# Output projection moved into the layers' stage, its gate's sums formed in the mixing stage, and four tiles leading each layer in units of four row blocks of two tiles

## What is computed

```python
# end of the first block
y = concatenate([ssd_out_norm(...), gdn_out_norm(...)])
h_lat = h_lat + gate_l * rms_norm(y @ w_out, post_w)     # gate_l: the last third of silu(c) @ w_ada + b_ada
# second block, two layers
for l in range(2):
    h = rmsnorm(x, norm_g[l])
    proj = h @ w_in[l]                                   # 7168 columns: v, q, k, g, mq, mg, c, x, s, b tiles
    ...
    x = x + concatenate([y_a, y_d, y_m]) @ w_out[l]
```

## Time and profile before

| what | value |
|---|---|
| median of three runs | 3634.65 us (3633.68 to 3636.38) |
| the profiled execution | 3634.55 us, its span 3632.8 us |
| TensorE busy | 3439.6 us, 95% |
| VectorE / ScalarE / GpSimd busy | 47% / 41% / 9% |
| mean granted TensorE clock | 0.972 |
| recurrent stage's last TensorE work ends | 1530.3 us |
| output projection's products | 1551.0 to 1740.0 us |
| first product of layer 1 / of layer 2 | 1797.1 / 2715.9 us |

### The profile page before, as it was taken

One profiled execution on the slowest core, in us unless ns is written; L12 is line 12 of the kernel. 1 busy time (PEld: TensorE's weight loads), 2 busy tenths in 40 slices (PEclk: granted clock), 3 DMA queues, 4 the chain that ended last, 5 costly groups with the idle time before them and its releaser, 6 DMA issues.

```text
span 3632.8 us, 53291 instructions
## 1 busy us (share of the span) xinstructions
PE 3439.6 (95%) x21996; PEld 2811.6 (77%) x21996; DVE 1712.8 (47%) x2813; ACT 1480.5 (41%) x2296; POOL 318.0 (9%) x334
## 2 busy tenths in 40 slices
PE   7999999999978989799699999999999999999998
PEld 5888888888857878678377777887777777788787
DVE  7665564565525656544744444333234444443422
ACT  6564443344325353232365555222225555632211
POOL 0000230130003323100200000000100000000000
PEclk9999999999989999899799999999999999999999
DMA  9642332333440010165322222333432222233342
GB/s 375 209 143 61 91 101 71 86 105 102 126 163 25 15 49 26 46 212 203 136 87 75 81 83 85 103 99 99 145 104 81 81 81 81 76 104 96 96 139 81
DMA packets 150081, 383.39 MB, mean 106 GB/s; under 512 B 14257, under 2 KB 39089, under 8 KB 149841
## 3 DMA queue, kind: packets, MB, share of 16 engines
q1 hardware_dynamic: 138384, 338.44, 29.5%
q0 software_dynamic: 11456, 41.56, 3.3%
HBM read 350.38 MB, written 29.56 MB: 105 GB/s over the span
## 4 chain that ended last, share of the span: by engine, by line
PE 49%; DVE 1%; ACT 0%; issue 0%; DVEq 0%; POOL 0%; ACTq 0%
PE lay_acc L2478 42%; PE lay_nb L2494 1%; PE lay_sA L2533 1%; PE lay_ob L2551 1%; PE lay_om L2478 1%; PE lay_tb L2512 1%; DVE lay_four L2895 1%; DVE lay_u_lo L2899 0%; PE lay_om L2561 0%; DVE lay_wlo L2774 0%; DVE lay_u_lo L2904 0%; ACT lay_whi L2615 0%; PE lay_tb L2518 0%; PE lay_sA L2541 0%; PE lay_sB L2541 0%
## 5 line engine op out<-in xcount | busy, mean ns | idle before, releaser
L2478 PE MATMUL lay_acc<-lay_u_hi,lay_whi 128*128 128x512 f32 x2240 | 898.7, 401 | 0.0
L2478 PE MATMUL lay_acc<-lay_u_hi,lay_wlo 128*128 128x512 f32 x2240 | 875.4, 391 | 0.0
L2478 PE MATMUL lay_acc<-lay_u_lo,lay_whi 128*128 128x512 f32 x2240 | 874.2, 390 | 0.0
L2774 DVE TENSOR_TENSOR lay_wlo<-lay_stage,lay_whi 128x1024 fp32r<-128x1024 f32 x288 | 360.9, 1255 | 528.6 <-ACT lay_whi L2615 527.9
L2478 PEld LDWEIGHTS lay_acc<-lay_u_hi,lay_whi 128*128 128x128 f32 x2240 | 422.0, 188 | 106.9 <-issue 21.9
L2615 ACT ACTIVATE lay_whi<-lay_stage 128x1024 fp32r<-128x1024 f32 x288 | 303.0, 1054 | 477.1 <-PE lay_acc L2478 417.1
L2478 PEld LDWEIGHTS lay_acc<-lay_u_lo,lay_whi 128*128 128x128 f32 x2240 | 422.2, 188 | 91.1 <-issue 6.7
L2478 PEld LDWEIGHTS lay_acc<-lay_u_hi,lay_wlo 128*128 128x128 f32 x2240 | 421.6, 188 | 89.9
L842 PE MATMUL proj_lat<-proj_u_hi,proj_whi 128*128 128x512 f32 x832 | 339.2, 408 | 8.2 <-DVE proj_wlo L1058 8.2
L842 PE MATMUL proj_lat<-proj_u_hi,proj_wlo 128*128 128x512 f32 x832 | 327.0, 393 | 0.0
L842 PE MATMUL proj_lat<-proj_u_lo,proj_whi 128*128 128x512 f32 x832 | 326.4, 392 | 0.0
(11 more groups left out here) (413 smaller groups left out, 5459.5 us busy)
## 6 DMA issues: line engine op xcount, KB each, us to landing
lay_stage<-units_dram SPq DMA_DIRECT2D x288, 512.0 KB, 3.6
tokens_unit_stage<-in_units_dram SPq DMA_DIRECT2D x212, 256.0 KB, 2.7
front_stage<-in_w_ada_dram SPq DMA_DIRECT2D x64, 512.0 KB, 5.5
front_stage<-in_w_kv_dram SPq DMA_DIRECT2D x32, 512.0 KB, 4.7
out_stage<-in_w_out_dram SPq DMA_DIRECT2D x16, 1024.0 KB, 5.6
out_wg<-in_w_ada_dram POOLq DMA_DIRECT2D x32, 512.0 KB, 4.8
tokens_x_sb<-scr_arow SPq DMA_DIRECT2D x32, 256.0 KB, 4.5
tokens_x_sb<-in_xT_dram SPq DMA_DIRECT2D x4, 1536.0 KB, 10.4
```

What stands on the lines that cost most here:

```text
L2478: mm = pe.matmul(bank_of(t)[:], w[:, i % SLOTS, k, :], u[:, kt, :], start=(kt == n == 0), stop=(kt == KT - 1 and n == 2))
L2774: dve.tensor_tensor(wlo[:, i % SLOTS, :, :], stage[:, i % DEEP, :, :], whi[:, i % SLOTS, :, :].bitcast(F32), ALU.subtract)\
```

## The change

**The output projection goes into the stage of the layers.** `Stream` and `project_out` are gone. `layers` begins with 32 units of w_out in the layers' own ring and form (eight row blocks of one tile, 512 KB), the first four as a pair, tile by tile in four banks in turn. y comes in six pieces, x in four, all on SyncE; the first units and y's first row blocks alternate in its queue.

**The sums over channels change.** ScalarE squares a tile (`take_out`), VectorE adds the squares of all tiles but the last (`o_sum`), and TensorE meets them once at the end. The sum of squares of the new x is no longer taken from x: with x' = x + rs * (gamma * res) it is x^2 + 2 rs * (x * gamma * res) + rs^2 * (gamma * res)^2, each summed over channels; the first is known from `front` (its reciprocal root `rs`, squared and inverted), the other two are added up tile by tile during the projection (`cross_out`, `square_gated`). So the factor for the first layer's norm is ready before x' is.

**The gate's sums** are formed in the mixing stage, 64 pieces of 256 KB, at units that `gate_at` names, outside the two windows in which heads are worked on; a DRAM scratch carries them to the layers' stage.

**The lead of each layer.** The first four tiles form eight units, each four row blocks by two tiles. All four tiles take a row block before the next one is touched. Units 3 to 7 are split between row blocks of u (`LEAD_SPLITS`). The first head starts four units later.

In the first layer VectorE's list holds, per row block, x', u and u's low part in turn; x' is stored by GpSimd's queue.

The diff, cut to its core:

```diff
 def project_and_scan(...):
+    free = [i for i in range(30, NU) if not any(HEAD0[g] <= i < HEAD0[g] + 4 * HG for g in range(SSD_G))]
+    for q in range(D // 512):
+        for kt in range(KT):
+            gate_at[free.pop(0)] = (q, kt)
+        gate_stored_at[max(gate_at) + 1 + DEEP] = q
+        free = free[2:]
+    gate_load_at = {i + DEEP - 1: q * KT + kt for i, (q, kt) in gate_at.items()}
...
+                def load_gate(j):                                       # SyncE
...
+                    if j >= 2:
+                        sp.wait_ge(g_used, j - 1)
+                    sp.dma_start(wg[:, j % 2, :], dr.w_ada[2 * D // 512 + q, kt // 2, :, kt % 2 * 512:(kt % 2 + 1) * 512]).then_inc(g_loaded[j % 2], 16)
...
+                def add_gate(q, kt):                                    # VectorE
+                    dve.wait_ge(g_loaded[j % 2], 16 * (j // 2 + 1))
...
+                        op = dve.scalar_tensor_tensor(out=gacc[:], in0=wg[:, j % 2, :], scalar=c_lat[:, kt:kt + 1], in1=gacc[:], op0=ALU.mult, op1=ALU.add)
...
-def project_out(nc, dr, name, w_v, src_x, dst_x, cols, c_lat, x, x_rs):
...
-PAIRS = (0, N_IN)
+LEAD_TILES, LEAD_K = 4, 4
+LEAD_UNITS = LEAD_TILES * KT // 8
+UNITS = [(2 * (_j % 2), _j // 2) for _j in range(LEAD_UNITS)]
...
+O_UNITS = [(0, 0), (1, 0), (0, 1), (1, 1)] + [(n, h) for n in range(2, KT) for h in range(2)]
...
+    LEAD_SPLITS = {1: (3,), 6: (4, 5), 10: (6, 7)}
+    HEAD_AT[0] += 4
...
+                load_y(0)                                               # SyncE
+                load_out_unit(0)
+                load_y(1)
+                load_out_unit(1)
...
+                for g in range(4):
+                    sp.wait_ge(y_left, 4 * g + 4)
+                    sp.dma_start(x[:, 4 * g:4 * g + 4, :], dr.xT...).then_inc(x_loaded[g], 16)
+                for g in range(NX):
+                    if g + DEEP < NX:
+                        load_out_unit(g + DEEP)
...
+                def lead(l):                                            # TensorE
+                    for part in range(KT // LEAD_K):
+                        i = NU * l + 2 * part
+                        pe.wait_ge(lo_ready, NX + i + 2)
+                        for k in range(LEAD_K):
+                            kt = part * LEAD_K + k
+                            pe.wait_ge(u_left, 2 * KT * l + kt + 1)
+                            for t in range(LEAD_TILES):
+                                at, b = (i + t // 2) % SLOTS, t % 2 * LEAD_K + k
+                                for n, (w, u) in enumerate(((whi, u_hi), (whi, u_lo), (wlo, u_hi))):
+                                    mm = pe.matmul(bank_of(t)[:], w[:, at, b, :], u[:, kt, :], ...)
...
+                def out_sums():
+                    pe.matmul(nb[:], ones[:], o_sum[:], start=True, stop=False)
+                    pe.matmul(ob[:], ones[:], cross_sum, start=True, stop=False)
+                    pe.wait_ge(o_squared, KT)
+                    pe.matmul(nb[:], ones[:], o_sq, start=False, stop=True).then_inc(o_summed, 1)
+                    pe.matmul(tb[:], ones[:], gated_sum, start=True, stop=False)
+                    pe.matmul(ob[:], ones[:], cross, start=False, stop=True)
+                    pe.matmul(tb[:], ones[:], gated, start=False, stop=True).then_inc(cross_done, 1)
...
+                def make_var():                                         # VectorE
+                    dve.scalar_tensor_tensor(out=var, in0=o_rs, scalar=0.5, in1=tb[:], op0=ALU.mult, op1=ALU.mult)
+                    dve.tensor_tensor(var, var, ob[:], ALU.add)
+                    dve.scalar_tensor_tensor(out=var, in0=var, scalar=2.0 / D, in1=o_rs, op0=ALU.mult, op1=ALU.mult)
+                    dve.tensor_tensor(var, var, rs[:, 0:LAT], ALU.add)
+                    dve.tensor_scalar(var, var, EPS, None, ALU.max).then_inc(var_ready, 1)
...
+                cross_out(KT - 1)
+                make_var()
+                add_out(0)
+                split(LEAD)
+                add_out(1)
+                dve.wait_ge(x_rs_ready, 1)
+                for k in range(KT + 1):
+                    make_u(0, [k])
+                    if k + 2 < KT:
+                        add_out(k + 2)
+                    for j in LEAD_SPLITS.get(k, ()):
+                        if j > LEAD:
+                            split(j)
...
-                        make_u(1, range(KT + 1))
+                        for k in range(KT + 1):
+                            make_u(1, [k])
+                            for n in LEAD_SPLITS.get(k, ()):
+                                split(i + n)
```

612 lines of the change are left out of this document (312 added, 300 removed).

## The result

The changed kernel takes **3594.83 us** (median of 4 runs, 3591.45 to 3599.52); the kernel before, in the same session, 3634.16 (3633.55 to 3636.38). The ratio is 0.9892, with a 95% interval of 0.9874 to 0.9909: 39 us less. The forecast was 3577, 58 us less; the measured time lies in its range of 3564 to 3600, and outside the narrower bounds of 3566 to 3590, to which it gave 70%.

What follows compares the result with a forecast made beforehand. TensorE, busy 95% of the span, was taken as the bound, so its work or pauses had to shrink. Terms -6.2 - 5.9 - 37.4 - 9.1 + 0 + 1 = -57.6 took about 3634.6 to 3577 us, range 3564 to 3600.

Steps and rivals of the forecast that it cites:

- rival 2: Opening of the projection bound by transfers, first product and unit 4 later: 3588 us, or 3591 with low clock; 13%.
- Start of the projection: From the recurrent stage's end to the projection's first product: smaller first loads let it start 6.2 us earlier.
- Inside the projection: Projection's products: sums of squares go to VectorE, with one new SyncE wait of 2.3 us; 5.9 us less.
- Behind the projection: From T, the projection's last product's end, to first layer's four tiles complete: start at T+17.1, level pace; 37.4 us less.
- Second layer: Second layer's first product to four tiles complete: VectorE well ahead, no pause for splits; 9.1 us less.
- Head 0: Head 0 of each layer runs four units later, eight before head 1: +1 us for both layers (0 to 6).
- Gate's sums: Mixing stage: 64 loads and VectorE adds, covered by TensorE's three units of lead; 0 us (bounds 0 and 5).
- (1): TensorE's clock stays low through the first layer's lead, all 192 products 0.43 us apart: 3609 us; 9%.
- rival 3: Mixing stage: adds wait for their own loads and hold VectorE; 3622 to 3679 us without overlap; 5%, 3% ending slower.
- (4): Behind the projection the sum for the second root is still awaited as long as before: 3612 us; 3%.

Runs made afterwards that it cites:

- Experiment 4: Changed kernel with SyncE asking for the projection's unit 4 + g ahead of x's piece g, not after all four pieces; 3589.7 us, ratio 0.9878.
- Experiment 1: Changed kernel with the second turn of the memory's values moved from unit 8 of each layer to unit 11; 3577.52 us, ratio 0.985.
- Experiment 2: Changed kernel with each piece for the gate's sums asked for one unit earlier in the mixing stage; 3590.69 us, ratio 0.9881.
- Experiment 5: Changed kernel with the gate's 16 columns formed ahead of the projection's first product, not behind unit 5; 3595.86 us, ratio 0.9893.
- Experiment 10: Changed kernel with memory's second turn at unit 11, gate pieces asked for one unit earlier, projection units 4 to 7 ahead of x's pieces; 3577.65 us, ratio 0.9843.
- Experiment 12: Changed kernel with only the memory's second turn at unit 11 and the projection's units 4 to 7 ahead of x's pieces; 3582.94 us, ratio 0.9852.
- Experiment 9: Changed kernel with two tiles in each layer's lead, then the other two, splits behind row blocks 6, 10, 14 and 16; 3606.03 us, ratio 0.9919.
- Experiment 3: Changed kernel with only 4 of the gate sums' 64 pieces loaded and added, so the gate differs; 3590.03 us, ratio 0.9882.

## Why the prediction was right, and where it was not

That the range held is partly luck: head 0's term came out 5.4 us beyond its own bound, and the time 5 us beyond the narrower bounds; the room up to 3600 had been made for rival 2 as well, which didn't come.

**Start of the projection** (-6.2): -6.0. Right, and by its chain: ScalarE rounds the second unit at 1546.67, 12.3 us behind the end of the recurrent stage (12.2 in the working), and the rounding and the split follow. That the small units are the reason was not tried alone.

**Inside the projection** (-5.9): -3.2. The new wait on SyncE was named and priced at 2.3 us, and was 3.25; its price rested on landings by my estimate. Another 1.6, the rest of the term's error, were not in the working: behind the gate's columns eight products stand 0.43 us apart (1592.3 to 1595.7), the granted clock's lower level. Experiment 4 takes the wait away and 3.9 us with it.

**Behind the projection** (-37.4): -38.1. The chain was right step by step: the layer starts at T + 16.9 (17.1), VectorE's row blocks follow at 2.7 us (2.75), the second pair of splits makes TensorE wait 1.8 with 1.7 of slow products (2.7 + 1). The last 1.7 fit the sum by chance: in experiments 1, 2, 4, 5, 10 and 12 the same lead had no slow products behind that wait, and was complete at T + 64.8 or 64.9. Experiment 9 shows that the level pace was the right reason, 6 what the interleaving pays.

**Second layer** (-9.1): -9.7. Right.

**Head 0** (+1, bounds 0 to 6): **+11.4**. This is the step that failed, in "I take +1 us for both layers (0 to 6), since the later heads stand eight apart too". I looked at the distance of the heads, on TensorE's units, and not at the one bank that the turns share. Three turns stand behind three successive units, as before, but ScalarE's list in that place now has three changes of table and not two, and needs longer than a unit for its share. Experiment 1 shows it: one number changed, and 10 to 11 us are back. What is left with that edit is 675.0 us from four tiles to the pause in each layer, 1.7 above the two stretches before (674.3 and 674.0), near the +1 of the forecast; the scores' wait of 1.1 us in each layer, which the kernel before didn't have, stands in it.

**Gate's sums** (0, bounds 0 to 5): +4.1 at the end of the recurrent stage, +4.9 at the end of the mixing stage in this profile and 3 on average. The bound held, the value taken did not: "TensorE has three units of lead, so I take 0" overlooked that VectorE's list has copies on which TensorE waits without that lead. It was rival 3 in small: the add does wait for its own load (55 us in 34 waits), but TensorE's own waits grew at two copies only, by 2.1 us in all, and slower work follows (the eight products at 847.92 take 1.70 us, 1.08 before). Experiments 2 and 3 show that the loads are the cause.

**The rivals.** (1) Slow clock through the lead: no; ten products at the start and eight after the wait of 1.8. In experiment 9, with a dozen waits between 0.5 and 2.2 us in the lead, slow products follow after two of them (2.17 and 1.87) and full rate after the other ten, after a wait of 2.16 as well. The section of the Trainium skill that the prediction weighed (TensorE: Matmul & The Clock Gate, HAM oscillation) describes a kernel whose bursts of products are shorter than the waits for DMA between them, and each burst starts slow. Here TensorE waits for VectorE, and mostly for less than the burst takes (in experiment 9 some 1.1 us between bursts of 1.7), so that case is not tested; the prediction's wider reading, a fall behind each pause, did not come true for these waits. (2) Transfers at the opening: only the wait for unit 4. (4) The second root is not awaited as before: the layer starts at T + 16.9.
